# Scores of a gated linear recurrence: each chunk's 128x128 matmul as four matmuls of 32 stationary columns

## The chip, the cores and the metric

The kernel runs on one core of one Trainium2 chip. The metric is the device time of one execution in microseconds (us), the median of several runs. The program has 2017 lines of Bass code in which each engine's order and each wait is written out by hand: TensorE (PE), VectorE (DVE), ScalarE (ACT), GpSimd (POOL), and SyncE (SP), which issues the DMAs.

## The reference, cut to what matters

The whole model layer is one launch: RMSNorm, an input projection, a spatial gating mixer, a bidirectional gated linear recurrence with 8 heads, two merges, an output projection, a router, 16 experts and a last norm, for 1280 tokens (256 of a prompt and 1024 of a sample). The change touches the recurrence alone:

```python
def step(S, inp):
    qt, kt, vt, gt = inp
    G = jnp.cumsum(gt, axis=2)
    o_inter = jnp.einsum('bhtk,bhkv->bhtv', qt * jnp.exp(G), S)
    D = G[:, :, :, None, :] - G[:, :, None, :, :]
    decay = jnp.exp(jnp.where(tri, D, -jnp.inf))
    A = jnp.einsum('bhtk,bhtsk->bhts', qt, decay * kt[:, :, None, :, :])
    o = o_inter + jnp.einsum('bhts,bhsv->bhtv', A, vt)
```

It is done in both directions of time. A is the matrix of scores between the tokens of a chunk; each score carries the product of the gates between its two tokens.

## The kernel before, in words

In the recurrence (function `hgrn2`, stage name `hg`) the 1280 tokens are NT = 10 chunks of 128, and a head's q, K and gates lie with 128 features on the partitions and tokens on the free axis. The scores of a chunk are a 128x128 matrix (keys on the partitions, queries on the free axis) and are built in eight steps. Step 0, DIAG, multiplies `k_sum` by `q`; only the diagonal of the result is used. Steps 1 to 7 (LEVELS = 7) double a block: at level j a block has b = 2^(j-1) tokens, each pair of neighbouring blocks is crossed, and of the 128x128 result only the two b x b off-diagonal squares of each pair of blocks are used. The helper `crossed` makes the moving operand, which takes for the queries of one block of a pair `Q_f` and of the other `Q_b`, by strides.

In `pe_step` each of these steps is one float32 matmul per chunk: 128 stationary columns (keys), 128 moving columns (queries), with all 128x128 results written to PSUM (`bank_cols(base, c)`, tile `hg_G`). Steps alternate between PSUM banks 0 to 2 and 3 to 5. A float32 matmul is two records in the trace, each a weight load (PEld) and a matmul (PE): a step of 10 chunks shows x20. I call one load with its matmul a pair.

Three engines go round in a ring for each level. PE makes the step; DVE then (`dve_level`) multiplies Q by the block totals for the next level (L739, two instructions), copies K (`dve_copy`, L688) and merges the used squares into `A` by a mask (`dve_merge`, L727, three instructions); POOL (`pool_level`, L677, four instructions) multiplies K by the totals. PE's step j+1 waits for Q of level j, for K of level j and for the merge of step j-1.

Beside this PE has the projections, 5 tiles of 128 output columns per head, in PARTS = 4 parts each (`W.multiply`, L174 to L176, 24 pairs of 320 moving columns, part by part). `pe_round` sets the order: part n, then step n of the recurrence, for n = 0 to 19; steps are numbered DIAG 0, levels 1 to 7, transposes of K 8 and 9, STATE 10, OUT 11 and ONES 12, and from 13 on there are parts alone. The round of heads 0 to 6 is a loop (`pe.Fori(0, HEADS - 1)`); head 7 is written out behind it, with 4 parts only. Line 544 (`pe_values`), at a round's end, transposes the values into `hg_G` and is where the banks are first used.

Of the kernel before, what the change touches and what calls it, by code (L numbers as in the profile page):

```python
# [26 lines left out]
P = 128  # L27
# [4 lines left out]
T = T_PROMPT + T_SAMPLE  # L32
# [354 lines left out]
def crossed(both, row, t0, n, b):  # L387


    ap = both[:]  # L390
    return bass.AP(tensor=ap.tensor, offset=ap.offset + t0, ap=[list(ap.ap[0]), [2 * b, n // (2 * b)], [row + b, 2], [1, b]])
# [7 lines left out]
def hgrn2(nc, C, w_in, h_hi, h_lo, yb_dram, next_tile):  # L399
# [13 lines left out]
    with Stage(nc, "hg") as st:  # L413
        W = WeightStream(st, len(order), C.first_tile)
        q, vT, v, so, A, Kt_f, Kt_b = (st.sb(n, [P, T]) for n in ("q", "vT", "v", "so", "A", "Kt_f", "Kt_b"))
        f_f, f_b, tot_f, tot_b = (st.sb(n, [P, T]) for n in ("f_f", "f_b", "tot_f", "tot_b"))
        Q = st.sb("Q", [P, 2, T])
        Q_b, Q_f = Q[:, 0, :], Q[:, 1, :]
# [8 lines left out]
        k_sum, sq, rt, y = Kt_f, tot_f, tot_b, Kt_b  # L427
        G = st.ps("G", [P, 6, 4, P])
        Gc = G[:].rearrange("p b c t -> p (b c) t")

        def K_at(j):

            return (K_even, K_odd)[j % 2]
# [7 lines left out]
        def bank_cols(base, c):  # L441
            return Gc[:, 4 * base + c, :]

        def spans(base):
# [3 lines left out]

        names = ("v_ready", "gates_ready", "Q_ready", "K_ready",
                 "tot_ready", "k_sum_ready", "K_copied", "A_merged", "gla_step", "v_step", "Kt_ready", "S_ready", "sq_ready",  # L450
                 "rt_ready", "y_ready", "y_stored", "A_clear", "so_used", "silu_ready")
        s = {n: st.sem(n) for n in names}
        STEPS = 13
        DIAG, KTF, KTB, STATE, OUT, ONES = 0, 8, 9, 10, 11, 12
# [6 lines left out]
        def tiles_with(g):  # L461
            return [(g, TGO)] + [(g + 1, t) for t in (TQ, TZF, TZB, TI)]
# [6 lines left out]
        def sp_round(sp, r, done, first=False):  # L469

            for t, c in enumerate(order):
                if not (first and t == 0):
                    W.load(sp, r, t, cols(w_in, c + r * P))
                if t == 0 and done is not None:
                    store(sp, done)

        def store(sp, g):
            sp.wait_ge(s["y_ready"], NY * (g + 1) + CREDIT)
            st.stand(sp)
            sp.dma_start(yb_dram[bass.ds(g * P, P), :], y[:]).then_inc(s["y_stored"], 16)  # L480
# [57 lines left out]
        def pe_values(pe, r):  # L538

            for b in range(2):  # L540
                pe.wait_ge(W.bank_free[b], PARTS // 2 * (W.per * r + TI + 1) + CREDIT)
            pe.wait_ge(s["y_ready"], NY * r + CREDIT)
            for c in range(NT):
                mm = nc.tensor.transpose(bank_cols(0, c), vT[:, c * P:(c + 1) * P], C.ident[:])
            mm.then_inc(s["v_step"], 1)

        def act_values(act, r):
            act.wait_ge(s["v_step"], r + 1 + CREDIT)
            act.wait_ge(s["gla_step"], STEPS * (r - 1) + OUT + 1 + 2 * STEPS)
            nc.scalar.activation(v[:].rearrange("p (c t) -> p c t", t=P), Gc[:, 0:NT, :], ACT.Copy).then_inc(s["v_ready"], 1)  # L550

        def gla_at(g, step):
            return STEPS * g + step + 1 + 2 * STEPS

        def pe_step(pe, g, j):
            base = 3 * (j % 2)
            if j == DIAG:
                pe.wait_ge(s["v_ready"], g + 1)
                pe.wait_ge(s["k_sum_ready"], g + 1)
                for c in range(NT):  # L560
                    t = slice(c * P, (c + 1) * P)
                    mm = nc.tensor.matmul(bank_cols(0, c), k_sum[:, t], q[:, t], start=True, stop=True)  # L562
            elif j <= LEVELS:
                pe.wait_ge(s["Q_ready"], NQ * g + 2 * j + 2 * NQ)
                if j == 1:
                    pe.wait_ge(s["rt_ready"], g + CREDIT)
                    pe.wait_ge(s["gates_ready"], 6 * (g + 1))
                else:
                    pe.wait_ge(s["K_ready"], LEVELS * g + j - 1 + 2 * LEVELS)
                    pe.wait_ge(s["A_merged"], 8 * g + j - 1)  # L570
                b = 1 << (j - 1)

                for c in range(NT):
                    mm = nc.tensor.matmul(bank_cols(base, c), K_at(j)[:, c * P:(c + 1) * P], crossed(Q, T, c * P, P, b),
                                          start=True, stop=True)
            elif j in (KTF, KTB):
                pe.wait_ge(s["A_merged"], 8 * g + j - 1)
                pe.wait_ge(s["K_ready"], LEVELS * g + LEVELS + 2 * LEVELS)
                k = (K_f, K_b)[j == KTB]
                for c in range(NT):  # L580
                    mm = nc.tensor.transpose(bank_cols(base, c), k[:, c * P:(c + 1) * P], C.ident[:])
            elif j == STATE:
                pe.wait_ge(s["Kt_ready"], 2 * g + 2)
                for n, (Kt, c) in enumerate([(Kt_f, c) for c in state_f] + [(Kt_b, c) for c in state_b]):
                    t = slice(c * P, (c + 1) * P)
                    mm = nc.tensor.matmul(Gc[:, n, :], Kt[:, t], v[:, t], start=True, stop=True)
            elif j == OUT:
                pe.wait_ge(s["S_ready"], 16 * (g + 1))
                pe.wait_ge(s["A_merged"], 8 * g + 8)
                pe.wait_ge(s["Q_ready"], NQ * g + NQ + 2 * NQ)  # L590
                for c in range(NT):
                    t = slice(c * P, (c + 1) * P)
                    terms = [(v[:, t], A[:, t])]
                    if c not in firsts_f:
                        terms.append((S_f[:, c, :], Q_f[:, t]))
                    if c not in firsts_b:
                        terms.append((S_b[:, c, :], Q_b[:, t]))
                    for n, (lhs, rhs) in enumerate(terms):
                        mm = nc.tensor.matmul(bank_cols(0, c), lhs, rhs, start=(n == 0), stop=(n == len(terms) - 1))
            else:  # L600
                pe.wait_ge(s["sq_ready"], g + 1)
                for a in range(0, T, 512):
                    z = min(a + 512, T)
                    mm = nc.tensor.matmul(G[:, 3 + a // 512, :, :].rearrange("p c t -> p (c t)")[:, 0:z - a],
                                          C.ones[:], sq[:, a:z], start=True, stop=True)
            mm.then_inc(s["gla_step"], 1)
# [182 lines left out]
        with st.block() as block:  # L789

            @block.sync
            def _(sp):
                sp.sem_inc(s["y_stored"], 16 * CREDIT)
                W.sp_credit(sp)
                sp_round(sp, 0, None, first=True)
                sp_round(sp, 1, None)
                with sp.Fori(2, HEADS) as r:
                    sp_round(sp, r, r - 2)
                W.load(sp, HEADS, 0, next_tile)
                store(sp, HEADS - 2)  # L800
                store(sp, HEADS - 1)
                sp.wait_ge(s["y_stored"], 16 * (HEADS + CREDIT))

            @block.scalar
            def _(act):
                W.act_credit(act)
                act.sem_inc(s["rt_ready"], CREDIT)
                act_round(act, tiles_before, None)
                with act.Fori(0, HEADS - 1) as g:
                    act_round(act, tiles_with(g), g)  # L810
                act_round(act, tiles_last, HEADS - 1)

            @block.gpsimd
            def _(pool):
                W.pool_credit(pool)
                pool.sem_inc(s["K_ready"], 2 * LEVELS)
                nc.gpsimd.memset(A[:], 0.0).then_inc(s["A_clear"], 1)
                pool_round(pool, tiles_before, None)
                with pool.Fori(0, HEADS - 1) as g:
                    pool_round(pool, tiles_with(g), g)  # L820
                pool_round(pool, tiles_last, HEADS - 1)

            @block.tensor
            def _(pe):
                W.pe_credit(pe)
                pe.sem_inc(s["gla_step"], 2 * STEPS)
                pe.sem_inc(s["v_step"], CREDIT)
                pe_round(pe, tiles_before, None)
                with pe.Fori(0, HEADS - 1) as g:
                    pe_round(pe, tiles_with(g), g)  # L830
                pe_round(pe, tiles_last, HEADS - 1)

            @block.vector
            def _(dve):
                dve.sem_inc(s["Q_ready"], 2 * NQ)
                dve.sem_inc(s["y_ready"], CREDIT)
                dve.sem_inc(s["so_used"], CREDIT)
                dve.sem_inc(s["silu_ready"], CREDIT)
                dve_round(dve, 0, None)
                with dve.Fori(0, HEADS - 1) as g:  # L840
                    dve_round(dve, g + 1, g)
                dve_round(dve, None, HEADS - 1)
# [1175 lines left out]
```

## Time and profile before

| | us |
|---|---|
| median of 3 runs (2846.04 to 2851.55) | 2849.87 |
| the profiled execution's own time | 2844.18 |
| its span, first to last instruction | 2842.4 |
| PE busy in the span | 2596.3 |
| PE weight loads busy | 2548.4 |
| DVE busy | 1519.1 |
| POOL busy | 670.5 |

The span is the time between the first and the last instruction of the profiled execution; its own time has 1.8 us more around it. Busy times of PE come from records that overlap and whose ends are modelled, so the cost of a matmul in a stream is read from the distance of starts: in a merged row of n records, its length less one record's, divided by n-1. The mean granted clock of TensorE over the span is 0.958 of full speed.

### The profile page before, as it was taken

The numbers are of one execution on the slowest core, as the hardware profiler recorded it, in microseconds if no ns is written. First come the engines' busy times: TensorE is split into PE (matmuls) and PEld (weight loads), VectorE is DVE, ScalarE is ACT, GpSimd is POOL, SyncE is SP. The second block draws the span as 40 slices with busy tenths as digits, with TensorE's granted clock in tenths as the row PEclk, the third lists the DMA queues.
The fourth block names the chain that finished last, engine by engine and source line by source line (L and its number), as shares of the span: only waits on it lengthen the run. The fifth ranks groups of instructions, "written<-read, shape, count | busy, mean of one in ns | idle before, by whom it ended". The sixth has DMA issues, their size and how long they took to land. (4 is left out here: it accounts for less than half of the span.)

```text
span 2842.4 us, 49715 instructions
## 1 busy us (share of the span) xinstructions
PE 2596.3 (91%) x18702; PEld 2548.4 (90%) x18702; DVE 1519.1 (53%) x2298; ACT 962.7 (34%) x1569; POOL 670.5 (24%) x502
## 2 busy tenths in 40 slices
PE   5999899999999999999859997955999999999993
PEld 4999799999999999999859997935999999999993
DVE  4123300035755755755631112156889889889894
ACT  4222311122122122122121102142665665655653
POOL 1321311133523523523522113112010010010110
PEclk7999999999999999999879997976999999999997
DMA  3112321210110100110023215064788788788774
GB/s 112 30 36 89 127 72 48 65 38 16 47 31 15 46 31 15 46 31 15 17 92 99 90 61 193 15 251 148 255 264 278 255 264 277 246 275 270 253 243 165
DMA packets 332493, 349.58 MB, mean 123 GB/s; under 512 B 12048, under 2 KB 309008, under 8 KB 332432
## 3 DMA queue, kind: packets, MB, share of 16 engines
q1 hardware_dynamic: 326288, 327.79, 34.7%
q0 software_dynamic: 6144, 20.98, 3.5%
q8 instruction: 39, 0.64, 0.1%
q14 instruction: 22, 0.18, 0.0%
HBM read 301.54 MB, written 47.19 MB: 123 GB/s over the span
## 5 line engine op out<-in xcount | busy, mean ns | idle before, releaser
L1772 PE MATMUL ex_out<-ex_xT,ex_w_hi 128*128 128x320 f32 x2048 | 533.0, 347 | 2.3 <-DVE ex_xT L1610 2.3
L1773 PE MATMUL ex_out<-ex_xT,ex_w_lo 128*128 128x160 f32 x2048 | 484.0, 236 | 0.0
L1592 DVE TENSOR_TENSOR ex_w_lo<-ex_raw,ex_w_hi 128x1024 fp32r<-128x1024 f32 x374 | 455.0, 1217 | 0.4
L1586 ACT ACTIVATE ex_w_hi<-ex_raw 128x1024 fp32r<-128x1024 f32 x384 | 387.2, 1045 | 26.8 <-PE ex_out L1773 13.9
L1773 PEld LDWEIGHTS ex_out<-ex_xT,ex_w_lo 128*128 128x128 f32 x2048 | 392.6, 192 | 0.0
L1772 PEld LDWEIGHTS ex_out<-ex_xT,ex_w_hi 128*128 128x128 f32 x2048 | 385.8, 188 | 2.9 <-DVE ex_xT L1610 2.4
L1772 PE MATMUL ex_out<-ex_hT,ex_w_hi 128*128 128x320 f32 x1024 | 279.1, 351 | 0.2
L174 PE MATMUL hg_proj<-trunk_h_hi,hg_w_hi 128*128 128x320 f32 x768 | 244.6, 318 | 0.0
L1773 PE MATMUL ex_out<-ex_hT,ex_w_lo 128*128 128x160 f32 x1024 | 241.8, 236 | 0.0
L175 PE MATMUL hg_proj<-trunk_h_lo,hg_w_hi 128*128 128x320 f32 x768 | 237.4, 309 | 0.0
L176 PE MATMUL hg_proj<-trunk_h_hi,hg_w_lo 128*128 128x320 f32 x768 | 237.4, 309 | 0.0
L1773 PEld LDWEIGHTS ex_out<-ex_hT,ex_w_lo 128*128 128x128 f32 x1024 | 195.5, 191 | 0.0
L1721 POOL DMA_INDIRECT x_sample<-ex_y_s,ex_out_s x16 | 25.8, 1615 | 717.1 <-ACT ex_y_p L1666 717.1
L1772 PEld LDWEIGHTS ex_out<-ex_hT,ex_w_hi 128*128 128x128 f32 x1024 | 192.1, 188 | 2.3 <-DVE ex_hT L1646 0.6
L174 PE MATMUL hg_proj<-trunk_h_hi,trunk_w_hi 128*128 128x320 f32 x512 | 161.3, 315 | 5.3 <-POOLq L199 5.3
L175 PE MATMUL hg_proj<-trunk_h_lo,trunk_w_hi 128*128 128x320 f32 x512 | 158.9, 310 | 0.0
L176 PE MATMUL hg_proj<-trunk_h_hi,trunk_w_lo 128*128 128x320 f32 x512 | 158.8, 310 | 0.0
L174 PEld LDWEIGHTS hg_proj<-trunk_h_hi,hg_w_hi 128*128 128x128 f32 x768 | 144.5, 188 | 0.2
L175 PEld LDWEIGHTS hg_proj<-trunk_h_lo,hg_w_hi 128*128 128x128 f32 x768 | 144.5, 188 | 0.2
L176 PEld LDWEIGHTS hg_proj<-trunk_h_hi,hg_w_lo 128*128 128x128 f32 x768 | 144.2, 188 | 0.0
L159 POOL TENSOR_TENSOR trunk_w_lo<-trunk_w_raw,trunk_w_hi 128x1024 fp32r<-128x1024 f32 x31 | 76.1, 2456 | 280.7 <-ACT trunk_w_hi L153 280.7
L727 DVE COPY_PREDICATED hg_A<-all_mask,hg_G 128x512 f32<-128x512 uint8 (+1 forms) x192 | 107.4, 631 | 32.5 <-PE hg_G L562 28.6
(318 smaller groups left out, 6226.9 us busy)
## 6 DMA issues: line engine op xcount, KB each, us to landing
ex_raw<-in_w_exp_gate_dram SPq DMA_DIRECT2D x64, 1024.0 KB, 4.9
ex_raw<-in_w_exp_up_dram SPq DMA_DIRECT2D x64, 1024.0 KB, 4.9
ex_raw<-in_w_exp_down_dram SPq DMA_DIRECT2D x64, 1024.0 KB, 5.5
trunk_w_raw<-in_w_in_dram SPq DMA_DIRECT2D x48, 512.0 KB, 4.2
hg_w_raw<-in_w_in_dram SPq DMA_DIRECT2D x16, 512.0 KB, 3.9
ya<-gm_ya SPq DMA_DIRECT2D x8, 640.0 KB, 3.4
m_a<-ma_m SPq DMA_DIRECT2D x8, 640.0 KB, 3.4
yb<-hg_Kt_b SPq DMA_DIRECT2D x8, 640.0 KB, 5.1
```

The source lines that it names most:

```text
L159: nc.gpsimd.tensor_tensor(self.lo[s][:], self.raw[rs][:], self.hi[s][:].bitcast(F32), ALU.subtract).then_inc(self.lo_ready, 1)
L174: nc.tensor.matmul(out, self.hi[s][:, k, :], x_hi[:, k, c], start=(k == 0), stop=False)
L175: nc.tensor.matmul(out, self.hi[s][:, k, :], x_lo[:, k, c], start=False, stop=False)
L176: mm = nc.tensor.matmul(out, self.lo[s][:, k, :], x_hi[:, k, c], start=False, stop=(k == KC - 1))
L727: cp = nc.vector.copy_predicated(A[:, c0 * P:c1 * P].rearrange("p (c t) -> p c t", t=P), C.mask[:, j, :].unsqueeze(1).broadcast_to([P, n, ...
L1586: nc.scalar.activation(w_hi[t % RING][:], raw[p % RAW][:, :, c:c + P], ACT.Copy).then_inc(s["w_hi_ready"], 1)
L1592: ops.tensor_tensor(w_lo[t % RING][:], raw[p % RAW][:, :, c:c + P], w_hi[t % RING][:].bitcast(F32), ALU.subtract).then_inc(lo_done(e, t)[0 ...
L1721: nc.gpsimd.indirect_dma_start(x3[1], bass.IndirectOffsetOnAxis(ap=out_s[:], axis=0), y_s[:], None, compute_op=ALU.add).then_inc(s["added_ ...
L1772: nc.tensor.matmul(bank[:, 0:2 * SLOTS], w_hi[i][:, k, :], B[:, k, :], start=(k == 0), stop=False)
L1773: mm = nc.tensor.matmul(bank[:, SLOTS:2 * SLOTS], w_lo[i][:, k, :], B[:, k, 0:SLOTS], start=False, stop=(k == KC - 1))
```

## The change

A chunk's matmul in DIAG and in levels 1 to 7 becomes four, one for each quarter of 32 keys. Each has 32 stationary columns and writes the 32 PSUM partitions of its keys. Only those queries move that can have a used score with these keys: the quarter's own 32 in DIAG and up to level 5 (2b at most 32), the neighbouring 32 in level 6, and the other half's 64 in level 7. In levels 6 and 7 the moving columns lie in one row of `Q_b` or `Q_f`. The rest of a chunk's 128x128 square is not written any more; DVE clears `G` once at the start of the stage and PE waits for that before its first use. The masks, the merges and all else stay.

```diff
-                 "rt_ready", "y_ready", "y_stored", "A_clear", "so_used", "silu_ready")
+                 "rt_ready", "y_ready", "y_stored", "A_clear", "G_clear", "so_used", "silu_ready")
...
+            pe.wait_ge(s["G_clear"], 1)
             pe.wait_ge(s["y_ready"], NY * r + CREDIT)
...
+        TILE = 32
+
+        def square(base, c, i, at, n):
+
+            return bank_cols(base, c)[i * TILE:(i + 1) * TILE, at:at + n]
+
+        def partners(j, c, i):
+
+            b = 1 << (j - 1)
+            if 2 * b <= TILE:
+                return i * TILE, TILE, crossed(Q, T, c * P + i * TILE, TILE, b)
+            second = i * TILE // b % 2 == 0
+            at = (i * TILE // (2 * b)) * 2 * b + (b if second else 0)
+            return at, b, (Q_b, Q_f)[second][:, c * P + at:c * P + at + b]
...
                 for c in range(NT):
-                    t = slice(c * P, (c + 1) * P)
-                    mm = nc.tensor.matmul(bank_cols(0, c), k_sum[:, t], q[:, t], start=True, stop=True)
+                    for i in range(P // TILE):
+                        own = slice(c * P + i * TILE, c * P + (i + 1) * TILE)
+                        mm = nc.tensor.matmul(square(0, c, i, i * TILE, TILE), k_sum[:, own], q[:, own], start=True, stop=True)
...
-                b = 1 << (j - 1)
-
                 for c in range(NT):
-                    mm = nc.tensor.matmul(bank_cols(base, c), K_at(j)[:, c * P:(c + 1) * P], crossed(Q, T, c * P, P, b),
-                                          start=True, stop=True)
+                    for i in range(P // TILE):
+                        at, n, rhs = partners(j, c, i)
+                        own = slice(c * P + i * TILE, c * P + (i + 1) * TILE)
+                        mm = nc.tensor.matmul(square(base, c, i, at, n), K_at(j)[:, own], rhs, start=True, stop=True)
...
+                nc.vector.memset(G[:], 0.0).then_inc(s["G_clear"], 1)
```

The first place is on PE in the loop of the recurrence, around level 1 (the names are out<-moving,stationary; x10 counts the float32 matmuls, each of which is two pairs). Before:

```order
L174 MATMUL hg_proj<-trunk_h_hi,hg_w_hi 128x320
L175 MATMUL hg_proj<-trunk_h_lo,hg_w_hi 128x320
L176 MATMUL hg_proj<-trunk_h_hi,hg_w_lo 128x320
L564 ISA
L566 REGISTER_ALU
L567 REGISTER_ALU
L574 MATMUL hg_G<-hg_Q,hg_K_odd 128x128 x10
L169 REGISTER_ALU
```

and now:

```order
L174 MATMUL hg_proj<-trunk_h_hi,hg_w_hi 128x320
L175 MATMUL hg_proj<-trunk_h_lo,hg_w_hi 128x320
L176 MATMUL hg_proj<-trunk_h_hi,hg_w_lo 128x320
L581 ISA
L583 REGISTER_ALU
L584 REGISTER_ALU
L592 MATMUL hg_G<-hg_Q,hg_K_odd 32x32 x40
L169 REGISTER_ALU
```

Nothing has moved past anything: 40 matmuls stand where 10 stood, behind the same waits and ahead of the same projection part.

The second place is level 7 on PE in the same loop. Before:

```order
L176 MATMUL hg_proj<-trunk_h_hi,trunk_w_lo 128x320
L564 REGISTER_ALU
L569 REGISTER_ALU
L570 REGISTER_ALU
L574 MATMUL hg_G<-hg_Q,hg_K_odd 128x128 x10
L167 REGISTER_ALU
L169 REGISTER_ALU
```

and now:

```order
L176 MATMUL hg_proj<-trunk_h_hi,trunk_w_lo 128x320
L581 REGISTER_ALU
L586 REGISTER_ALU
L587 REGISTER_ALU
L592 MATMUL hg_G<-hg_Q,hg_K_odd 32x64 x40
L167 REGISTER_ALU
L169 REGISTER_ALU
```

Here the 40 matmuls have 64 moving columns each.

## Rows read from the trace of the kernel before

**Rows 1.** Head of the page, and busy time by engine.
```profile
span 2842.4 us, 49715 instructions
...
PE 2596.3 (91%) x18702; PEld 2548.4 (90%) x18702; DVE 1519.1 (53%) x2298; ACT 962.7 (34%) x1569; POOL 670.5 (24%) x502
```

**Rows 2.** Busy time by stretch: one head's turn of the loop.
```profile
core 0: us, PE busy (x) PEld busy (x) DVE busy (x) ACT busy (x) POOL busy (x), PEclk, DMA share, GB/s
...
944.22:1051.09 106.87, 105.33 (x762) 103.27 (x761) 64.34 (x88) 26.17 (x44) 40.84 (x33) 1.00 0.10 31
```

**Rows 3.** Timeline of PE, steps of that head: start, length, merged records.
```profile
944.22 2.39 PE L562 MATMUL hg_G<-hg_q,hg_Kt_f 128*128 128x128 f32 x20
949.97 3.49 PE L574 MATMUL hg_G<-hg_Q,hg_K_odd 128*128 128x128 f32 x20
956.83 2.56 PE L574 MATMUL hg_G<-hg_Q,hg_K_even 128*128 128x128 f32 x20
962.76 2.39 PE L574 MATMUL hg_G<-hg_Q,hg_K_odd 128*128 128x128 f32 x20
...
980.62 2.49 PE L574 MATMUL hg_G<-hg_Q,hg_K_even 128*128 128x128 f32 x20
```

**Rows 4.** Instructions of L574: duration ns min/median/max, first and last start.
```profile
L574 PE MATMUL hg_G<-hg_Q,hg_K_odd x640: 270/275/582, 629.4 to 1415.5; 128*128 128x128 f32 x160
```

**Rows 5.** Waits of PE from 600 to 1460 us: total, times, longest.
```profile
PE hg_G L599 <- DVE hg_S_b L756: 8.5, 8, 4.1
PE hg_G L574 <- DVE hg_Q L739: 7.9, 4, 2.3
PE hg_G L544 <- ACT hg_vT L507: 5.0, 7, 0.7
```

**Rows 6.** Timeline of DVE, the first level, levels 4 to 5, and the stage's start.
```profile
953.60 0.83 DVE L739 TENSOR_TENSOR hg_Q<-hg_Q,hg_f_f 128x640 f32<-128x640 f32 x1 [5.10 <-PE hg_G L574]
...
971.02 2.55 DVE L739 TENSOR_TENSOR hg_Q<-hg_Q,hg_tot_f 128x640 f32<-128x640 f32 x1 [2.19 <-PE hg_G L574]
...
979.01 1.39 DVE L739 TENSOR_TENSOR hg_Q<-hg_Q,hg_tot_b 128x640 f32<-128x640 f32 x1
...
591.20 0.95 DVE L527 TENSOR_SCALAR hg_f_f<-hg_f_f,all_one_minus_lb,all_lb 128x1280 f32<-128x1280 f32 x1 [35.74 <-ACT hg_K_odd L513]
```

**Rows 7.** Timeline of PE, step ONES; durations in ns (min/median/max) of the same.
```profile
1018.76 2.31 PE L604 MATMUL hg_G<-hg_tot_f,all_ones 128*128 128x512 f32 x6
...
L604 PE MATMUL hg_G<-hg_tot_f,all_ones x6: 379/592/592, 1018.8 to 1020.7; 128*128 128x512 f32 x4, 128*128 128x256 f32 x2
```

**Rows 8.** Timeline of PE and PEld, short transposes, and a narrow stationary operand (stationary rows*columns).
```profile
2053.16 0.68 PE L1744 MATMUL ex_X<-all_ident,ex_x_p 32*128 32x32 f32 x8
...
2053.16 0.57 PEld L1744 LDWEIGHTS ex_X<-all_ident,ex_x_p 32*128 32x128 f32 x8 [0.17 <-issue]
...
1894.46 0.79 PE L1432 MATMUL rt_turned<-all_ident,rt_router 16*128 16x16 f32 x10 [0.51 <-DVE rt_router L1461]
...
1897.65 0.60 PE L1438 MATMUL rt_turned<-all_ident,rt_prob_s 128*32 128x128 f32 x4
```

**Rows 9.** Durations in ns (min/median/max) of the transposes L1744.
```profile
L1744 PE MATMUL ex_X<-all_ident,ex_x_p x128: 220/222/311, 1953.4 to 2736.5; 32*128 32x32 f32 x128
```

**Rows 10.** DMA queues from 628 to 714 us, the loop's first turn: packets, MB, share.
```profile
q8 instruction: 6, 0.10, 0.5%
```

**Rows 11.** DMA queues from 730 to 1371 us, the loop's other turns: all there are.
```profile
q1 hardware_dynamic: 31024, 19.14, 9.8%
q14 instruction: 1, 0.01, 0.0%
```

**Rows 12.** Timeline of PE, last head, levels 5 and 6; clock in that stretch.
```profile
1399.06 3.65 PE L574 MATMUL hg_G<-hg_Q,hg_K_odd 128*128 128x128 f32 x20 [2.29 <-DVE hg_Q L739]
1405.01 4.64 PE L574 MATMUL hg_G<-hg_Q,hg_K_even 128*128 128x128 f32 x20 [2.31 <-DVE hg_Q L739]
...
1400.00:1416.00 16.00, 12.04 (x56) 11.45 (x56) 10.12 (x17) 0.00 (x0) 9.59 (x10) 0.51 0.00 0
```

## The prediction

> **What bounds the kernel now.** I read the page's head first. PE is busy for 2596.3 us of a span of 2842.4 and its weight loads for nearly as long; DVE has 53% and POOL 24% [rows 1]. Busy PE records overlap, so I went on to the stretch view of one head's turn of the recurrence loop: 106.9 us, 105.3 of them PE, 64.3 DVE, 40.8 POOL, at full clock [rows 2]. The waits say the same from the other side. From 600 to 1460 us PE waited for Q at L574 for 7.9 us, all in 4 waits, and for the states at L599 and the values at L544 for 8.5 and 5.0 us [rows 5]. In the loop PE is the bound and its steps stand on the path one behind the other: what a step gets longer, the head gets longer. A gain is less sure. DVE waits 5.10 us for PE at the first level, but at levels 4 and 5 one of its multiplies of Q takes 2.55 us instead of 0.83, and from 971.02 to 980.40 (the end of the second multiply of level 5) it has no gap, while PE's level 6 starts at 980.62 [rows 3, 6]. What PE saves between those two points, DVE takes back.
>
> **What a step costs now.** In a merged row of n records the distance of starts is its length less one record, by n-1. A record of a 128-column matmul is 0.275 us [rows 4]. DIAG and level 3 are 2.39 us for 20 records: (2.39-0.275)/19 = 0.111 us per pair. Level 1, whose moving operand jumps at each column, has 0.169, level 2 0.120; from level 3 on the stride costs nothing [rows 3]. Levels 4 to 7 are like level 3. A head's eight steps are thus 20 x (6 x 0.111 + 0.120 + 0.169) = **19.1 us**.
>
> **What a pair costs with 32 and 32 columns.** The trace has none, so I bound it.
> The moving columns: in ONES, 4 records of 512 and the first of 256, 2304 columns, take 2.31-0.38 = 1.93 us, 0.00084 us each [rows 7]. 128 columns are 0.107, and the 0.004 above that in a pair of 0.111 belongs to no column. 32 columns are 0.027, with the 0.004 it is 0.031. This is exactly a quarter of the columns, but four times the pairs: four pairs have as many moving columns as one had, and pay the 0.004 four times. The lower bound for pairs one behind the other is 0.027.
> The stationary columns: a narrow stationary operand alone saves nothing. L1438, 32 stationary and 128 moving columns, has (0.60-0.27)/3 = 0.11 [rows 8].
> The upper bound: the nearest rows with few moving columns are transposes. L1744 (32 moving, 128 stationary) has loads (0.57-0.14)/7 = 0.061 apart, L1432 (16 moving) matmuls (0.79-0.21)/9 = 0.064 [rows 8, 9]. Half the moving columns gave no less, so there either the load of 128 columns or a floor per pair holds them.
> I take 0.034, near the lower bound, since the new load is a quarter as wide: 0.031 and 0.003 for the change of quarter at every second pair (a guess between 0 and the 0.03 that lead up to 0.061).
> The page "TensorEngine Tiling (Array Packing)" of the Trainium skill, section "Instruction Overhead", says that a matmul of 1 column takes as long as one of 60, about 60 cycles, and warns against tiling a dimension that is small already. By that rule the 32-column pair costs 0.025 at 2.4 GHz and the sum below would come down to +24 with the lower bound of the rows; its warning is the one against this change.
>
> **The sum per head.** 480 pairs of DIAG and levels 2 to 6 by 0.034: 16.3. Level 2's stride, a quarter of 0.009 on 80 pairs: 0.2. Level 1, 0.034 and a quarter of 0.058: 80 x 0.0485 = 3.9. Level 7 has 64 columns, 0.054+0.004+0.003 = 0.061 by 80: 4.9; it moves twice the columns it did. Together 25.3 against 19.1, **+6.2 us**, of which level 7 alone is +2.7. All of it lies on PE's path in the loop. In the last head PE waits for DVE at each late level [rows 12], but DVE waits for PE's step there first, so a longer step counts there too. Two of its levels run at a granted clock of 0.51, 1.2 of 2.4 GHz, where columns cost double; that may add 3 us and is left to the range. Eight heads: **+49.4 us**.
>
> **Code.** One turn of the loop has 762 recorded pairs [rows 2] and would have 762+480 = 1242. In the loop's first turn q8 fetched 6 pieces, 0.10 MB, in 86 us (16 KB for about 17 us of work, some 120 pairs), and in the other turns nothing [rows 10, 11]. So 762 pairs, some 100 KB, stay in place; whether 165 KB do, no row shows. If not, each jump back (6 of them) waits for at least one piece: 0.5% of 16 engines' 86 us by 6 pieces is 1.1 us each [rows 10]. Bounds 0 and, at two pieces and an issue more, 4 us for each jump; I take one piece, 1.1: **+6.6 us**. The page "Runtime: NRT & Kernel Launch", section "Instruction fetch mechanics", of the Trainium skill gives PE room for 128 KiB of code and says a jump to a target outside it stalls. By that rule this body no longer stays; the trace agrees as far as 100 KB goes.
>
> **At no cost.** The clearing of G: DVE idles 35.74 us up to L527 at 591.20, at the start of the stage [rows 6], and PE first needs G at the end of that round. A memset of 3072 columns would have to last over ten times a 2.55 us multiply to be seen. The merges, copies and POOL's multiplies stay as they are; masks hide the cleared squares.
>
> Sum: 49.4+6.6 = +56. The profiled execution took 2844.18 (its span and 1.8 around it), 5.7 under the median of the runs. 2849.9+56 = **2906 us**.
>
> **Rivals.**
> *Forecast: pairs one behind the other*, 0.029 to 0.045 per pair. With p for the 32-column pair a head's steps are 640p+3.5 us. 0.029 without refetch gives +3.0 a head, 2874; 0.045 with refetch +13.2 a head, 2962. Own range 2872 to 2962. For it speaks that every stream of PE in rows 3 and 7 goes by its columns. Chance 0.55.
> *The quarters run side by side (faster).* The four quarters write different partitions from different stationary columns; if PE streams one quarter while the next has begun, two at a time, the 25.3 become 12.7, -6.4 a head. DVE takes back level 5's saving, 2.22 less 80 x 0.017 = 0.9, as it has no gap there [rows 6]. 8 x -5.5 = -44, with the refetch -37: 2813; all four at a time would be nearer 2770. It decides below 0.024 us per pair on average (640p+3.5 = 19.1). Against it: the two records of a float32 matmul write the same quarter and must follow each other, and no stream in the trace goes faster than its columns. Chance 0.17. The page "TensorE: Matmul & The Clock Gate" of the Trainium skill, Part 3, reports 2.38 times for three column tiles at 512 moving columns; no row here shows it.
> *A floor per pair (much slower).* If the 0.061 to 0.064 of rows 8 are not the wide load but what any load with its matmul costs, all 640 pairs are 0.062: 39.7-19.1 = 20.6 a head, +165 and refetch: 3021. For it: 16 and 32 moving columns cost the same there. Against: they are runs of 8 and 10 behind a 128-column load. Chance 0.22. The same page of the Trainium skill, section "Back-to-back issue gap", has 62 ns per matmul with decoding in software; that would be this case.
> *It cancels*, a partial overlap against refetch and level 7: within 0.2%, 0.06.
>
> **How the numbers follow.** 0.2% of 2850 is 5.7 us, about what a measurement of this kernel can tell from no change. Slower: 0.55+0.22 = 0.77; faster 0.17; same 0.06. The range holds the forecast's own, the floor with its refetch at the upper bound (3021+17, so 3035), and the small overlaps down to 2825: outside are most of the full overlaps (0.12) and a floor above 0.063 (0.04).
>
> **What would show it.** A timeline of PE with levels 3 to 6 as x80, 2.7 to 2.8 us from the first to the next projection part, level 7 4.9, level 1 3.9; a turn of 113 us; pairs 0.034 apart, and no new waits for DVE. q8 with 10 pieces in each turn and a gap of PE at the start of a turn would show the refetch. Level 3 under 1.9 us, with PE waiting for DVE at level 5 or 6, shows the overlap; 5.0 us and all levels alike shows the floor. Forecast wrong: a turn under 108 or over 121 us.

## The result

The change is **faster**: 2839.63 us (median of 7 runs, 2833.28 to 2842.78) against 2849.65 us (7 runs on the same chip, 2844.95 to 2851.55). The ratio is 0.9969 [0.9959, 0.9978], 10 us or 0.3%. The forecast was 2906 us and slower. The time lies in its range (2825 to 3035), on the side of the rival "side by side"; that it does is luck, as the part on the forecast shows: the steps gained far more than the range allowed for, and other costs gave most of it back.

### The profile page after: what moved, and what is told of

It is laid out like the page before. It is cut to its first block and busy times, and to the rows that moved or that the text cites. A ratio compares the mean times of both kernels' runs of the same rounds, so it can differ in the third digit from the quotient of the medians.

```text
span 2836.8 us, 57398 instructions
## 1 busy us (share of the span) xinstructions
PE 2534.8 (89%) x22542; PEld 2473.4 (87%) x22542; DVE 1554.0 (55%) x2299; ACT 962.9 (34%) x1569; POOL 707.2 (25%) x502
## 5 line engine op out<-in xcount | busy, mean ns | idle before, releaser
L174 PE MATMUL hg_proj<-trunk_h_hi,hg_w_hi 128*128 128x320 f32 x768 | 250.3, 326 | 15.9 <-issue 15.9
L174 PE MATMUL hg_proj<-trunk_h_hi,trunk_w_hi 128*128 128x320 f32 x512 | 166.6, 325 | 5.3 <-POOLq L199 5.3
L174 PEld LDWEIGHTS hg_proj<-trunk_h_hi,hg_w_hi 128*128 128x128 f32 x768 | 148.7, 194 | 19.3 <-issue 17.3
L159 POOL TENSOR_TENSOR trunk_w_lo<-trunk_w_raw,trunk_w_hi 128x1024 fp32r<-128x1024 f32 x31 | 76.0, 2451 | 281.5 <-ACT trunk_w_hi L153 281.5
```

The lines of the kernel that those rows point to most:

```text
L159: nc.gpsimd.tensor_tensor(self.lo[s][:], self.raw[rs][:], self.hi[s][:].bitcast(F32), ALU.subtract).then_inc(self.lo_ready, 1)
L174: nc.tensor.matmul(out, self.hi[s][:, k, :], x_hi[:, k, c], start=(k == 0), stop=False)
```

## The profile after

The head of the page answers to [rows 1]: PE's busy time fell from 2596.3 to 2534.8 us with 3840 pairs more, 61.5 us less, of which the span shows 5.6. DVE and POOL are busy for 35 and 37 us more.

```profile
span 2836.8 us, 57398 instructions
...
PE 2534.8 (89%) x22542; PEld 2473.4 (87%) x22542; DVE 1554.0 (55%) x2299; ACT 962.9 (34%) x1569; POOL 707.2 (25%) x502
```

The timeline of PE in the same head as [rows 3], with the turn's start ahead of it (start, length, merged records, the idle time before and who ended it):

```profile
941.72 1.31 PE L545 MATMUL hg_G<-all_ident,hg_vT 128*128 128x128 f32 x10 [0.67 <-issue]
945.93 0.63 PE L174 MATMUL hg_proj<-trunk_h_hi,hg_w_hi 128*128 128x320 f32 x1 [2.90 <-issue]
946.36 0.47 PE L175 MATMUL hg_proj<-trunk_h_lo,hg_w_hi 128*128 128x320 f32 x1
...
949.07 0.31 PE L174 MATMUL hg_proj<-trunk_h_hi,hg_w_hi 128*128 128x320 f32 x1
...
950.93 0.90 PE L579 MATMUL hg_G<-hg_q,hg_Kt_f 128*32 128x32 f32 x80
...
960.18 0.90 PE L592 MATMUL hg_G<-hg_Q,hg_K_even 128*32 128x32 f32 x80
...
964.72 0.90 PE L592 MATMUL hg_G<-hg_Q,hg_K_odd 128*32 128x32 f32 x80
...
983.07 1.30 PE L592 MATMUL hg_G<-hg_Q,hg_K_even 128*32 128x32 f32 x80 [3.82 <-DVE hg_Q L756]
...
988.93 1.32 PE L592 MATMUL hg_G<-hg_Q,hg_K_odd 128*32 128x64 f32 x80
```

Three things are to be seen. **First**, a step of 80 pairs takes 0.90 us where 20 whole pairs took 2.39; level 7, with 64 moving columns, takes 1.32. A record of 32 columns still lasts about 0.20 us (next fence), so the pairs start (0.90-0.20)/79 = 0.009 us apart. The forecast had 0.034. **Second**, the first projection part of the turn now waits 2.90 us for "issue", which stood in no turn before, and the records behind it are 0.27 us apart and not 0.15. ("issue" is a wait for nothing that the profile shows.) **Third**, level 6 waits 3.82 us for VectorE's multiply of Q, where there was no wait.

Durations in ns (min/median/max) of the level steps, as [rows 4]:

```profile
L592 PE MATMUL hg_G<-hg_Q,hg_K_even x1920: 189/198/263, 638.5 to 1404.7; 128*32 128x32 f32 x192
```

The waits of PE from 600 to 1450 us (total, times, longest), as [rows 5]:

```profile
PE hg_G L592 <- DVE hg_Q L756: 35.0, 9, 4.8
PE hg_proj L174 <- issue: 15.9, 6, 2.9
PE hg_G L616 <- DVE hg_S_b L773: 8.5, 8, 4.1
PE hg_G L592 <- POOL hg_K_odd L694: 7.1, 9, 3.6
PE hg_G L592 <- POOL hg_K_even L694: 6.1, 8, 4.3
```

The wait for Q was 7.9 us in 4 and is 35.0 in 9. The wait for issue comes 6 times, once for each jump back of PE's loop. q8, the queue that carries code in pieces of some 16 KB, answers to [rows 11]; this is the stretch of 730 to 1371 us, in which it moved nothing before:

```profile
q8 instruction: 71, 1.16, 0.7%
```

The stretches of that turn (PE busy, its clock in the column before the last two): the whole turn from DIAG to the next DIAG, the turn's start ahead of DIAG, in it the 3.40 us with the lower clock around the end of the wait for issue, and the start of the next turn, which is the end of the first row.

```profile
core 0: us, PE busy (x) PEld busy (x) DVE busy (x) ACT busy (x) POOL busy (x), PEclk, DMA share, GB/s
950.93:1058.35 107.42, 99.01 (x1242) 95.08 (x1241) 68.62 (x88) 26.18 (x44) 46.68 (x34) 0.95 0.11 33
941.72:950.93 9.21, 6.31 (x35) 5.88 (x35) 3.35 (x14) 2.18 (x2) 5.60 (x4) 0.81 0.20 58
945.40:948.80 3.40, 2.87 (x11) 2.88 (x12) 0.00 (x0) 0.00 (x0) 3.40 (x2) 0.50 0.02 5
1047.94:1058.35 10.41, 7.77 (x35) 7.35 (x35) 3.35 (x14) 2.18 (x2) 6.80 (x5) 0.67 0.19 54
```

So the start of a turn, 4.67 us long before (939.55 to 944.22), now takes 9.21: 2.90 of waiting for issue, and from its last half microsecond on a granted clock of 0.50, the 1.2 of 2.4 GHz, for 3.4 us. At two of the six jumps, the next one among them, the clock stays there for 6.8 us, and the start takes 10.3 and 10.4 us; at the other four it takes 8.9 to 9.4.

Where a turn's time lies now, by the starts of its steps (us; the fourth turn of each kernel; the first two columns are the two kernels above, the other two are experiments told below):

| stretch | before | change | loop written out | and gate moved |
|---|---|---|---|---|
| DIAG to level 3 | 18.54 | 13.79 | 14.11 | 14.11 |
| level 3 to level 6 | 17.86 | 18.35 | 18.79 | 17.51 |
| level 6 to the next DIAG | 70.47 | 75.28 | 69.51 | 69.65 |
| turn | 106.87 | 107.42 | 102.41 | 101.27 |

The early levels keep what they save, 4.75 us. From level 3 to level 6 nothing is saved at all, although three steps there are some 1.5 us shorter each. The rest of the turn loses 4.8 us, and 10.41-4.67 = 5.7 us of loss lie at the jump back. This turn is one of the longer ones; the seven from the first DIAG to the last are 106.3 us in the mean, against 106.86 before, 3.9 of the 5.6 us that the span shows.

## Experiments: do the quarters run side by side?

The kernel before was run again beside each group of experiments (medians 2848.02, 2849.54 and 2847.16 us on three chips); each ratio is to the one beside it.

**same_quarter.** The same instructions, but all ten chunks of one quarter before the next quarter's.

```diff
-                for c in range(NT):
-                    for i in range(P // TILE):
+                for i in range(P // TILE):
+                    for c in range(NT):
```

> The changed kernel with its two loops in a step exchanged: all 10 chunks' first quarter, then all second quarters, and so on; the same 40 matmuls of a step. If the gain of a step comes from different quarters running side by side (theory A), matmuls of one quarter must follow each other: pairs 0.029 to 0.034 us apart as the prediction had it, a step 2.4 to 2.7 us, level 7 4.5 to 4.9, a turn 112 to 117 with the fetching, 2890 to 2920 in all. If short matmuls simply issue 0.009 us apart whatever they are, it stays at 2840.

Measured: 2897.25 us, ratio 1.0178 [1.0162, 1.0193]. The timeline of PE shows DIAG, level 1 and level 2 at

```profile
969.14 2.42 PE L579 MATMUL hg_G<-hg_q,hg_Kt_f 128*32 128x32 f32 x80
975.21 3.13 PE L592 MATMUL hg_G<-hg_Q,hg_K_odd 128*32 128x32 f32 x80
981.99 2.42 PE L592 MATMUL hg_G<-hg_Q,hg_K_even 128*32 128x32 f32 x80
```

(2.42-0.20)/79 = 0.028 us per pair: single starts are mostly 31 to 32 ns apart and come closer only around a change of quarter. The order alone makes 0.009 or 0.028 us. That is the forecast's "one behind the other", in size too (0.031 before its allowance); it holds for pairs of one quarter, and was wrong for this change, where a chunk's matmuls go through the quarters in turn. The body is as long as the change's and pays the same waits for issue (15.6 us in 6), so they don't make the difference of 58 us.

**wide_quarters_unrolled.** Quarters of 32 stationary columns, each with all 128 moving columns; PE's loop written out as below.

```diff
-                        mm = nc.tensor.matmul(square(0, c, i, i * TILE, TILE), k_sum[:, own], q[:, own], start=True, stop=True)
+                        mm = nc.tensor.matmul(square(0, c, i, 0, P), k_sum[:, own], q[:, c * P:(c + 1) * P], start=True, stop=True)
...
-                        at, n, rhs = partners(j, c, i)
+                        at, n, rhs = 0, P, crossed(Q, T, c * P, P, 1 << (j - 1))
```

> Quarters of 32 stationary columns as in the change, but each with all 128 moving columns instead of its own 32 (what they write outside the diagonal blocks is not read, so nothing else changes), PE's loop written out. Tells how the gain divides: quarters side by side, or fewer moving columns. If the quarters run side by side, whatever their moving columns, four pairs together take about as long as one whole pair, 0.11 us: a step of 80 pairs 2.2 us or so, and the whole about 2844 us, as the kernel before with its loop written out. If what counts is only the columns of one pair and each runs behind the other, a pair keeps 0.11 us, a step 8.9 us, and the whole is near 3280 us.

Measured: 2857.76 us, ratio 1.0041 [1.0025, 1.0056]. The timeline of PE:

```profile
950.09 2.39 PE L579 MATMUL hg_G<-hg_q,hg_Kt_f 128*32 128x128 f32 x80
956.13 3.58 PE L592 MATMUL hg_G<-hg_Q,hg_K_odd 128*32 128x128 f32 x80
```

80 quarter pairs of 128 columns take 2.39 us, exactly as 20 whole pairs do [rows 3]: all four quarters stream at once. In the single records the starts come in groups of four, 6 to 7 ns apart, and the next group 0.09 us behind, so a group takes 0.11 us, as one whole pair does. So the saving of the change is its fewer moving columns, and the fourfold count of pairs costs nothing because the four run together. The time is 14 us above my 2844: steps of equal length begin 6.04 us apart and not 5.75, so a step of quarters has some 0.3 us more around it than a whole one, 1.8 us a turn (108.3 against 106.47) and 13 in seven, which is nearly all of it. The change pays this too: its steps are 1.49 us shorter (2.39 to 0.90) and begin only 1.21 us closer. What the 0.3 us are was not tried.

**tile64 and unrolled_tile64.** Halves of 64 columns (`TILE = 64`), with PE's loop and with it written out.

> The changed kernel with two matmuls of 64 stationary and 64 moving columns for each chunk instead of four of 32. A turn has 762+160 = 922 pairs, by 135 bytes of code each 125 KB. Theory A: two halves overlap as the four quarters do, a step takes 1.1 to 1.3 us instead of 2.2 (before) and 0.75 (quarters of 32), and if the body stays in place no turn waits for code: 103 us a turn, total 2818 to 2825. Theory B: at levels 4 to 6 DVE and POOL bind as well, so 2835 to 2845 with nothing gained at a turn's start. If halves do not overlap: a step at 2.3 us or more, 2850.

> The kernel with halves of 64, with the loop over heads written out for PE. Theory A: no turn waits for code, all turns as the first one of the kernel with halves, 102.2 us, total 2850-7 x 6 = 2808 to 2815, no worse than quarters of 32 written out (2813), since DVE and POOL end the waits at levels 4 to 6 in both. Theory B' (halves save less, 1.2 us a step instead of 0.7, and all of that shows): 0.5 x 8 steps x 8 heads = 32 us more than the quarters, 2845.

Measured: 2849.66 us, ratio 1.0008 [0.9998, 1.0017], with the loop; 2810.45 us, ratio 0.9866 [0.9851, 0.9881], without. A step of 40 pairs takes 1.39 us: two halves of 64 columns, in 0.060 us together. That is slower than the quarters' 0.90 (which stream 32 columns a chunk). Written out, the whole is still as fast (2810.45 against 2812.98 us, with intervals that overlap). So once the steps are this short their length no longer decides. With the loop it is 10 us slower than the change and gains nothing. That is the time expected of halves that don't overlap, but the step shows that they do; its turns wait for issue too, 15.6 us in 6, and the 2818 to 2825 of theory A were missed.

## Experiments: what does the jump back cost?

**unrolled_after, and unrolled_before as its control.** PE's loop over the heads is written out, so that PE's code runs straight on.

```diff
-                with pe.Fori(0, HEADS - 1) as g:
+                for g in range(HEADS - 1):
```

> The changed kernel, with the loop over heads 0 to 6 written out for PE alone (7 copies of the same instructions, nothing jumps back). Theory A (the four quarters overlap, and what they save is given back at each jump back, where the longer body's code has to be fetched again): the turns 2 to 7 get as short as the first turn of the changed kernel, 102.7 us instead of 106.0 to 108.2, no wait of L174 for issue at a turn's start, TensorE at full clock there; 6 x 4 = some 24 us less than the changed kernel, 2816. Theory B (what the steps save is taken back by DVE and POOL at levels 4 to 6, and fetching is hidden): as the changed kernel, 2840.

> The control: the kernel before, with the same loop written out for PE. Its body stays in place, so both theories expect the turns at 106.9 us as they are and 2850 within 5 us; a gain here of 10 us or more would mean that writing the loop out helps by something else than the fetching of the longer body.

Measured: 2812.98 us, ratio 0.9883 [0.9868, 0.9899], with the change; 2844.0 us, ratio 0.9984 [0.9975, 0.9993], for the kernel before. All seven turns of unrolled_after take 102.4 to 102.5 us; with the loop the first took 102.65 and the six with a jump 106.0 to 108.2 (counted from one start of L545 to the next). The control's turns of 106.47 us and its 2844.0 are a little below what was expected of it (106.9, and 2850 within 5 us). The wait of L174 for issue is gone from its list of waits (600 to 1450 us):

```profile
PE hg_G L592 <- DVE hg_Q L756: 36.5, 15, 4.8
...
PE hg_G L592 <- issue: 5.5, 14, 0.5
```

The last row is new, two short waits in each turn, ahead of levels 3 and 5; where they come from was not traced.

The code was still fetched, 61 pieces from 730 to 1360 us (36 in the control), but without a wait at a turn's start; what costs is the jump back. The mean of the six turns is 106.9 us, so a jump costs 4.5 us, and six are the 27 us between the two kernels. The control's turns gained 0.4 too, so 4.1 a jump, 25 us in all, go to the longer body. I had put 1.1 us, upper bound 4.

**halves_level1, cut1 and cut12**: how long may the body be? Only level 1 in halves (780 pairs a turn), only level 1 in quarters (820), levels 1 and 2 in quarters (880); all else whole, the loop kept.

```diff
+        CUT = (1,)
...
+                    if j not in CUT:
+                        mm = nc.tensor.matmul(bank_cols(base, c), K_at(j)[:, c * P:(c + 1) * P], crossed(Q, T, c * P, P, 1 << (j - 1)),
+                                              start=True, stop=True)
+                        continue
```

> Halves of 64 at level 1 alone, all other levels whole, PE's loop over the heads as it was: the smallest lengthening of PE's loop body, 20 pairs of instructions more in 760. Theory (a body that grows past what stays in place is fetched anew at the jump back, 4 to 7 us each; with level 1 in quarters, 60 pairs more, that happened in two turns of seven): here in none, and level 1's step 3.5 to 1.9 us gives 1.6 us in each of 8 heads, so 2837 us against 2849.7. Rival (any lengthening brings the fetches): 6 x 4 us back, 2850 or above.

> Level 1 alone in quarters of 32, DIAG and levels 2 to 7 as 128x128 matmuls as before, with the loop as it was. A turn has 820 recorded pairs (760 before, 920 in the kernel with halves of 64, whose turns waited for code). Theory A (above some length between, the body is fetched anew in each turn): this one stays in place, level 1 takes 0.9 instead of 3.3 us, the turn 106.9-2.4 = 104.5, all seven turns alike, and the total 8 x -2.4 = -19: 2829 to 2832. If even this body is fetched again, the turns 2 to 7 are 3.5 to 7 us longer than the first and the total is above 2848.

> Levels 1 and 2 in quarters of 32, the rest as before: 880 recorded pairs in a turn. If this stays in place: levels 1 and 2 take 0.9 and 0.7 us instead of 3.3 and 2.4, the turn is 106.9-4.1 = 102.8 (DVE and POOL still have room at levels 2 and 3), total 2815 to 2820, the best with a loop. If it doesn't: first turn 102.8, the others 106 to 110, total 2835 to 2852. The two together place the length from which a turn fetches its code again.

| kernel | pairs a turn | time, ratio | turns |
|---|---|---|---|
| halves_level1 | 780 | 2837.96, 0.9966 [0.9954, 0.9978] | seven of 105.5 |
| cut1 | 820 | 2856.74, 1.0024 [1.0014, 1.0035] | five of 104.7, two of 110.35 |
| cut12 | 880 | 2857.17, 1.0023 [1.0012, 1.0034] | first 103.84, then 108.2 to 109.5 |

The waits of PE from 730 to 1371 us, first of cut1:

```profile
PE hg_proj L174 <- issue: 8.2, 2, 4.2
```

of cut12:

```profile
PE hg_proj L174 <- issue: 15.0, 6, 2.8
```

and of halves_level1, where the only wait for issue is a short one at L545 (the kernel before has it too, 0.7 us at most, there put down to ACT [rows 5]):

```profile
PE hg_G L545 <- issue: 4.0, 6, 0.7
```

q8 carries 1, 19 and 52 pieces in that stretch in halves_level1, cut1 and cut12, so the wait is one for code, and it comes with the length, not with the quarters: absent at 780 pairs, at two jumps at 820, at all at 880. A jump costs 5.7 us in cut1, 5.5 or so in cut12 and 6.8 in tile64 (109.2 against 102.4, unrolled_tile64's mean). cut1 is thus slower than the kernel before with shorter steps, and its profiled run, 2844.1, is its fastest (up to 2862.04). The other times fit up to three more stalls of 5.7 us, so how many jumps stall probably differs from run to run; only this run was traced. cut1 missed its 2829 to 2832 us and came out as its other case, above 2848, though not in all turns; cut12 lies above both of its ranges; halves_level1 met its 2837. With 20 pairs more instead of 480, halves_level1 brings as much as the whole change.

## Experiments: what takes the late levels' saving?

In the timeline of VectorE in unrolled_after, from level 5's copy on, no row waits until the last multiply of Q ends at 966.44, and PE's level 6 starts at 966.49:

```profile
958.23 2.54 DVE L705 COPY hg_K_even<-hg_K_rest 128x640 f32<-128x640 f32 x1 [0.79 <-POOL hg_K_odd L694]
960.69 1.68 DVE L744 COPY_PREDICATED hg_A<-all_mask,hg_G 128x512 f32<-128x512 uint8 x3
962.27 1.58 DVE L536 TENSOR_TENSOR hg_so<-hg_vT,hg_so 128x1280 f32<-128x1280 f32 x1
963.77 1.37 DVE L756 TENSOR_TENSOR hg_Q<-hg_Q,hg_tot_f 128x640 f32<-128x640 f32 x1
965.07 1.37 DVE L756 TENSOR_TENSOR hg_Q<-hg_Q,hg_tot_b 128x640 f32<-128x640 f32 x1
```

The head of this chain is released by GpSimd's product for the level's keys. So a level is now a ring of VectorE (copy, merge, two multiplies) and GpSimd, with PE's short step a small part of it.

The ring itself has become slower. The copy takes 2.54 us here and at most 0.50 at the other levels, and for nearly all of it GpSimd has its weight split under way:

```profile
958.04 2.38 POOL L159 TENSOR_TENSOR hg_w_lo<-hg_w_raw,hg_w_hi 128x1024 fp32r<-128x1024 f32 x1
```

In the change and in unrolled_after each of seven such copies starts 0.2 us behind the start of L159 and ends 0.2 us behind its end. In the kernel before it is a multiply of Q that stands beside L159 and takes 2.55 us [rows 6]. The multiplies of Q take 0.82 us with GpSimd idle and 1.36 (medians) beside its work; 10 of 128 lay beside it for over nine tenths of their time before, 71 of 128 in the change. GpSimd's multiplies of level 4, ahead of this L159, take 0.80 us twice and then, beside those of Q, 1.38 and 1.36. The shorter steps thus bring the work of the two engines together in time, and each holds the other up: of the change's 35 us more on VectorE, 20 are in the multiplies of Q and 15 in the copies, and of GpSimd's 37 us, 33 are in its multiplies for K. What this costs in the end was not measured by a run of its own.

L536, the output gate, isn't part of any level; it only stands there in VectorE's program.

**late_gate_unrolled, and late_gate_before as its control.** The gate multiply goes behind the last merge; PE's loop is written out in both.

```diff
-                    if j == PARTS:
-                        dve_output_gate(dve, g)
+                dve_output_gate(dve, g)
                 dve_states(dve, g)
```

> The changed kernel with the loop written out for PE, and with DVE's multiply of the output gate (L536, 1.58 us), which stands between the merge of level 4 and the multiplies of Q of level 5, moved behind the last merge. If DVE is what ends PE's waits at level 6 (3.7 us in each turn), that wait falls to about 2.1 us and the total by 8 x 1.6 = 13 against 2813: 2800. If POOL ends it (its four multiplies of K, or its weight split just before), the wait and the time stay: 2813.

> Control: the kernel before (whole levels), with PE's loop written out and VectorE's gate multiply moved as in late_gate_unrolled. Theory: with whole levels PE itself sets the pace of each level, and the ring of VectorE and GpSimd has slack, so that moving the multiply brings nothing: 2840 to 2846 us, as 2844.0 with the loop alone written out. Rival (the multiply's place was a cost of its own, whatever the levels): 15 us less, as it was with quarters (2812.98 to 2797.62), so about 2829 us.

Measured: 2797.62 us, ratio 0.9820 [0.9807, 0.9833], with quarters; 2836.67 us, ratio 0.9961 [0.9948, 0.9974], with whole levels. The same place in the timelines of late_gate_unrolled, of VectorE and of PE:

```profile
951.87 2.54 DVE L705 COPY hg_K_even<-hg_K_rest 128x640 f32<-128x640 f32 x1 [0.79 <-POOL hg_K_odd L694]
954.33 1.69 DVE L744 COPY_PREDICATED hg_A<-all_mask,hg_G 128x512 f32<-128x512 uint8 x3
955.91 0.91 DVE L756 TENSOR_TENSOR hg_Q<-hg_Q,hg_tot_f 128x640 f32<-128x640 f32 x1
956.75 1.37 DVE L756 TENSOR_TENSOR hg_Q<-hg_Q,hg_tot_b 128x640 f32<-128x640 f32 x1
...
958.83 0.89 PE L592 MATMUL hg_G<-hg_Q,hg_K_even 128*32 128x32 f32 x80 [2.28 <-DVE hg_Q L756]
```

PE's wait at level 6 is 2.28 us instead of 3.72, and the step behind it has its 0.89 us again instead of 1.30. In this turn the clock still falls, 1.5 us later (960.3 to 963.7); in three of the seven turns it doesn't, and these take 100.1 us where the others take 101.2. The move brings 15 us with quarters (18 by the ratios, 0.9883 to 0.9820). I had expected nothing of it with whole levels, and it brought 7 (2844.0 to 2836.67; 6.5 by the ratios, 0.9984 to 0.9961): the turns went from 106.47 to 106.11, 2.5 us in seven, and the last head, in which PE waits for VectorE at every late level [rows 12], took 73.3 us from the start of L544 to the end of ONES and now 72.1. The rest is not accounted for. So more than half of the gain needs the short steps; the control's expectation was a miss, and the slack that it gave the ring is there in the turns only in part, and not in the last head.

**late_gate_tile64**: halves, loop written out, gate moved.

> The two changes that each took time off, together: halves of 64 instead of quarters of 32, PE's loop over the heads written out, and VectorE's gate multiply moved from the middle of the levels to behind the last merge. Theory (quarters or halves side by side; the end of a level is then set by the ring of VectorE and GpSimd): the halves run at 1.39 us a step against 0.90, but only where PE bounds, and the ring took this difference back when PE's loop was written out (2810.45 against 2812.98 us). With the gate multiply gone from the ring, 2797.62 us was measured with quarters; here 2795 to 2800. Rival (PE's own length sets the time again once the ring is relieved): the halves' longer steps, 5 or so of 0.5 us a head, show as 2.5 us x 8 = 20 us more, 2815.

Measured: 2796.48 us, ratio 0.9827 [0.9813, 0.9840], the same as with quarters within the intervals, with 320 pairs a turn fewer. Its turns are 100.54 us; level 6 waits 1.00 us for Q. These two are the fastest of all kernels here, about 50 us or 1.8% under the kernel before and 42 under the change.

## Why the forecast was wrong, step by step

*"Quarter pairs follow one behind the other, 0.034 us each."* **This step failed**, and the sign hung on it: measured 0.009 us. same_quarter shows that the working for such a pair was right (0.028), and wide_quarters_unrolled that four quarters stream at once. The argument against the overlap, that the two records of a float32 matmul write the same quarter and must follow each other, was true only within a quarter; the other three fill the time. (How the two records of one matmul lie among those of the other quarters, the rows don't show.) And the rows "no stream goes faster than its columns" had no two pairs in different quarters, so they bore on nothing here.

*The sum of the steps.* Instead of +6.2 us a head, a turn without waits would lose 1.2 us in each of DIAG and levels 3 to 6 (5.75 from start to start is 4.54), 2.15 at level 1, 1.39 at level 2 and 0.9 at level 7: -10.4 a head, -83 us. That would have been near the rival's "all four at a time, nearer 2770". I had given the rival 0.17. Two small sums of the forecast are off as well, without weight for it: its +24 for the lower bound of the rows is what 0.029 us a pair and no refetch give, with the bound itself, 0.027, it is +13 without and +20 with the refetch; and 3021+17 is 3038.

*"What PE saves between those two points, DVE takes back."* Right in kind, too small in size: I charged level 5 alone, 0.9 us. In the change levels 3, 4 and 5 together save nothing (17.86 us before, 18.35 and 18.79 now) where they would save 3.6, so 4.1 and 4.5 us a head are taken back, and from level 6 to level 7 another 1.3 by the slow clock behind PE's wait (5.9 us where 4.54 would do). With the loop written out, 4.0 of the 10.4 us reach the turn (106.47 to 102.43), with the gate moved in both kernels 5.4 (106.11 to 100.75 in the mean).

*"Code: one piece, 1.1 us for each jump back."* That the longer body wouldn't stay in place was right, the price was not: 4.5 us, 4.1 without what the control shows, at or above my upper bound of 4. The term was built from the transfer of one piece alone. It leaves out that PE stands still for 2.4 to 2.9 us and runs at half clock behind that. The signs named beforehand (about 10 pieces in each turn, a gap at the turn's start) are there, 71 pieces in six turns.
The page "Runtime: NRT & Kernel Launch" of the Trainium skill, section "Instruction fetch mechanics", has room for 128 KiB on PE. By the 16 KB for some 120 pairs of [rows 10], an estimate, the first stalls, at 820 pairs, are at about 110 KB, and 780 pairs or 104 KB have none, so the trace agrees roughly and sets the limit somewhat lower. The same section of the Trainium skill has a taken branch stall when its target lies outside a window of two pages; by pages of 16 KB these runs show no such thing, since a body of 104 KB jumps back without a stall.

*"The clearing of G at no cost."* No wait for it stands in the trace after.

*The floor of 0.062 us for any pair* (0.22) fell: pairs start 0.009 us apart. What held the short transposes of [rows 8] was not tried.
The page "TensorE: Matmul & The Clock Gate" of the Trainium skill, Part 3, reports 2.38 times for three column tiles at 512 moving columns. These runs show 4.0 times for four at 128 (80 quarter pairs in the time of 20 whole ones), and 0.028/0.009, 3.1 times, at 32 moving columns. The 62 ns per matmul that the same page of the Trainium skill has for decoding in software ("Back-to-back issue gap"), and the 60 cycles of the Trainium skill's page "TensorEngine Tiling (Array Packing)", section "Instruction Overhead", an estimated 0.025 us at 2.4 GHz, are no lower bound where quarters alternate: the starts are 0.009 us apart.

**The account.** Of -83 us the ring of VectorE and GpSimd, with the slow clock behind its waits and the short waits for issue, takes back 6.4 us a head (5.9 in the last), 51 us, and the jumps 25: -7 is left, against 10 measured. Only the 83 is worked out beforehand; the 51 and the 25 are themselves read from turns with and without the loop, so that the sum closes says only that no large term is missing. The 25 are shown by writing out the loop; of the 51, moving the gate shows 8 to 11 as the ring's, and the rest is argued from the waits.

## What to carry to other kernels

Float32 matmuls of 32 stationary columns whose outputs lie in different quarters of the PSUM partitions run at once if they are issued in turn; the same ones ordered quarter by quarter run one behind the other (2839.63 against 2897.25 us). Before lengthening a loop body, count its instructions: past a limit, here between 780 and 880 pairs, every jump back stalls, for 4 to 7 us, and a smaller cut (halves at level 1) or a written-out loop may bring more than a full one. When a matmul step shrinks, look at once for the ring of other engines that sets the level's pace, move out what doesn't belong to it, and see which of their instructions now run beside each other and last longer.

## What was not expected of the hardware

- Four float32 pairs of 32 stationary columns and 128 moving columns, in four quarters, take together 0.11 us, as one whole pair: 80 of them 2.39 us.
- The stall at the jump is not proportional to the body: 820 pairs stall at two jumps for 5.7 us each, 1240 pairs at all six for 4.5.
- Around the end of each halt of 2.4 us or more at a jump, and of 3.7 or 3.8 us at level 6, the granted clock fell to 0.50, for 3.4 or 6.8 us (change and unrolled_after), so each such wait costs more than its length: 24 projection records took 5.0 us (945.93 to 950.93) where they have 0.147 us each at full clock, 3.5.
- VectorE's copy of 640 elements takes 2.54 us at level 5 and 0.48 at other levels, in the kernels with quarters or halves at all levels, other than same_quarter and wide_quarters_unrolled. Each of these slow copies runs beside GpSimd's L159, none of the fast ones does for more than 0.1 us; no run moved L159 away.
